# The last stage of a two-layer decoder step, turned into token rows before the scale and the residual instead of after them

## The reference, cut to what matters

```python
def rms_norm(x, g):
    xf = x.astype(jnp.float32)
    y = xf * lax.rsqrt(jnp.mean(xf * xf, axis=-1, keepdims=True) + NORM_EPS)
    return (y * g.astype(jnp.float32)).astype(x.dtype)
...
    o = rms_norm(o.astype(h.dtype), norm_g).reshape(B, T, GLA_VW) * jax.nn.silu(gate)
    h = h + rms_norm(o @ w_out, post_g)
    return h, st
```

## Time and profile before

| | us |
|---|---|
| three runs | 2061.0, 2062.63, 2062.9 (median 2062.63) |
| the profiled execution, its own time | 2063.2 |
| its span, first to last record | 2061.3 |
| PE busy / PEld busy in the span | 1959.9 (95%) / 1840.8 (89%) |
| DVE / ACT / POOL busy | 827.3 (40%) / 644.0 (31%) / 688.1 (33%) |
| mean granted TensorE clock | 0.967 of full speed |

### The profile page before, as it was taken

The page is one execution under the profiler, slowest core; times in us unless marked ns, Lnnn a source line. Parts: engine busy times, 40 slices in busy tenths (PEclk is TensorE's granted clock), DMA queues, the critical chain, the costliest instruction groups (busy, mean ns, idle before and its releaser), DMA issues.

```text
span 2061.3 us, 38375 instructions
## 1 busy us (share of the span) xinstructions
PE 1959.9 (95%) x14973; PEld 1840.8 (89%) x14973; DVE 827.3 (40%) x1478; ACT 644.0 (31%) x1158; POOL 688.1 (33%) x304
## 2 busy tenths in 40 slices
PE   6999999999999998999889999999999999989997
PEld 6998998899889987999779988988998899879996
DVE  5376337625742665100341454054316422650004
ACT  5232223222221233222342343334225332442122
POOL 2333332223323321545213314322341333225451
PEclk9999999999999999999999999998999899979998
DMA  5655245424533443522324352444244424533322
GB/s 167 200 159 153 73 118 159 127 82 136 157 94 95 142 142 98 171 84 83 91 91 124 113 168 79 123 138 150 75 121 154 134 72 138 180 138 103 101 83 83
DMA packets 357436, 252.53 MB, mean 123 GB/s; under 512 B 15136, under 2 KB 324785, under 8 KB 356721
## 3 DMA queue, kind: packets, MB, share of 16 engines
q1 hardware_dynamic: 316364, 186.75, 31.4%
q10 hardware_dynamic: 40900, 63.42, 9.2%
HBM read 213.62 MB, written 36.96 MB: 122 GB/s over the span
## 4 chain that ended last, share of the span: by engine, by line
PE 77%; DVE 10%; issue 6%; ACT 3%; SPq 2%; DMA 1%; POOL 1%; ACTq 0%; DVEq 0%; POOLq 0%
PE proj L990 64%; PE scratch L990 8%; PE score L990 2%; PE scratch L993 2%; DVE kv L1516 1%; DVE xlo L1388 1%; DVE probw L1544 1%; SPq L467 1%; SPq L459 1%; DVE ek L1787 1%; ACT ek L864 1%; POOL wlo L555 1%; DVE mix L1700 0%; DVE tz L1377 0%; DVE enew L1575 0%
## 5 line engine op out<-in xcount | busy, mean ns | idle before, releaser
L990 PE MATMUL proj<-xhi,wlo 128*128 128x268 f32 x4096 | 1198.0, 292 | 14.7 <-POOL wlo L555 6.3
L990 PE MATMUL proj<-xlo,whi 128*128 128x268 f32 x4096 | 1187.2, 290 | 0.0
L990 PE MATMUL proj<-xhi,whi 128*128 128x268 f32 x4096 | 1186.7, 290 | 0.0
L555 POOL TENSOR_TENSOR wlo<-wraw,whi 128x1024 fp32r<-128x1024 f32 x258 | 634.5, 2469 | 1133.7 <-ACT whi L621 1133.7
L990 PEld LDWEIGHTS proj<-xhi,wlo 128*128 128x128 f32 x4096 | 787.0, 192 | 32.9 <-issue 22.5
L990 PEld LDWEIGHTS proj<-xlo,whi 128*128 128x128 f32 x4096 | 786.4, 192 | 0.8
L990 PEld LDWEIGHTS proj<-xhi,whi 128*128 128x128 f32 x4096 | 783.7, 191 | 0.0
L621 ACT ACTIVATE whi<-wraw 128x1024 fp32r<-128x1024 f32 x258 | 265.1, 1047 | 383.3 <-PE proj L990 278.7
L1377 DVE TENSOR_TENSOR tz<-proj,rstd 128x536 f32<-128x536 f32 x72 | 51.4, 713 | 294.8 <-PE proj L990 294.4
L1695 DVE TENSOR_SCALAR mix<-proj,cols 128x536 f32 x32 | 24.8, 776 | 340.2 <-ACT te L627 179.5
L730 ACT ACTIVATE probw<-score,small 128x128 f32<-128x128 f32 (+3 forms) x64 | 33.2, 524 | 171.5 <-DVE small L1467 171.5
(11 more groups left out here) (267 smaller groups left out, 1747.6 us busy)
## 6 DMA issues: line engine op xcount, KB each, us to landing
wraw<-in_w_in SPq DMA_DIRECT2D x192, 512.0 KB, 4.0
wraw<-in_w_out SPq DMA_DIRECT2D x64, 512.0 KB, 4.0
kv<-in_cache_k SPq DMA_DIRECT2D x128, 128.0 KB, 2.3
kv<-in_cache_v SPq DMA_DIRECT2D x128, 128.0 KB, 2.3
sst<-in_state_gla ACTq DMA_DIRECT2D x32, 512.0 KB, 5.2
out<-sst ACTq DMA_DIRECT2D x32, 512.0 KB, 3.6
hbuf<-h_residual ACTq DMA_DIRECT2D x2, 4288.0 KB, 14.6
vb<-v_sample_rows ACTq DMA_DIRECT2D x32, 256.0 KB, 5.5
```

The costliest lines, as they stand in the source:

```text
L555: pool.tensor_tensor(wlo[:, slot, :, 0:width], wraw[:, kc, :, 0:width], whi[:, slot, :, 0:width].bitcast(F32), ALU.subtract).then_inc(s_lo, 1)
L990: return pe.matmul(out, lhsT, rhs, start=start, stop=stop, skip_group_check=True)
```

## The change

Three things change, all in the last stage of layer 1.

1. **Sums of squares per token row.** `token_sums` replaces `sum_squares(3)`: the squares are now the stationary operand (five groups of tokens) and one column of ones is the moving one, so that each token's sum lands on its own partition, in columns 0 to 4 of `score`. The ten matmuls (five from `acc`, five from `te`) add to what stands there: DVE zeroes the five columns beforehand. This `memset` stands in DVE's program behind the last `x_lo` of out1, and PE waits for it (s_zero) ahead of the whole projection. ACT forms Ln and Exp on 128 x 5 instead of 128 x 536.
2. **Transposes of raw data.** PE transposes both the unscaled output (`mix`) and the residual (`hbuf`), 20 pieces each, into a pair of banks for each piece, four pairs in turn. ACT copies the turned residual to the row buffer. The first two residual pieces are turned between the two halves of the sums; the other pieces follow as residual, output, residual, output.
3. **One DVE pass for each piece.** On the turned rows the scale is one value for each partition: `scalar_tensor_tensor`, row buffer = output x rstd + row buffer, 20 passes of 128 x 512. The 32 passes over channel blocks and the 20 result copies go.

```diff
@@ SP, result stores
-                sp.wait_ge(*result_read(i))
+                sp.wait_ge(s_res, i + 1)
@@ new helper
+        def pieces(i):
+            two = [(scratch[0][:], scratch[1][:]), (proj[1][:, 0, :], proj[1][:, 1, :]),
+                   (proj[0][:, 0, :], proj[0][:, 1, :]), (score[:, 0:512], score[:, 512:1024])]
+            return two[i % 4]
@@ ACT
             out_stage(3, N_OUT1, False)
-            finish_rms(3)
-            for i in RESULT_ACT:
+            def turned_h(i):
                 w = P if i % 5 < TT else TB
-                act.wait_ge(s_fT, i + 1)
+                act.wait_ge(s_fH, i + 1)
                 if i >= 15:
                     act.wait_ge(s_yout[1], 16 * 6)
-                act.copy(y_buffer(i)[0:w], banks[i % 8].rearrange("p (k e) -> p k e", k=4)[0:w]).then_inc(s_fa2, 1)
+                act.copy(y_buffer(i)[0:w], pieces(i)[1][0:w].rearrange("p (k e) -> p k e", k=4)).then_inc(s_hc, 1)
+            for i in range(2):
+                turned_h(i)
+            act.wait_ge(s_ss, 4)
+            chain.link(act.activation(stat[:, 2:7], score[:, 0:5], ACT.Ln, scale=1.0 / D, bias=eps))
+            act.activation(stat[:, 8:13], stat[:, 2:7], ACT.Exp, scale=-0.5).then_inc(s_rstd, 1)
+            for i in range(2, 20):
+                turned_h(i)
@@ PE
             for s in range(GH):
                 head(s)
+            pe.wait_ge(s_zero, 1)
             out_proj(N_OUT1, "out1")
-            sum_squares(3)
-            for i in range(20):
...
-                if i >= 8:
-                    pe.wait_ge(*result_read(i - 8))
-                for k in range(4):
-                    last = transpose(banks[i % 8][0:w, k * P:(k + 1) * P], mix[:, 4 * kq + k, tt * P:tt * P + w])
-                last.then_inc(s_fT, 1)
+            def token_sums(src, start):
+                for tt in range(TT + 1):
+                    w = P if tt < TT else TB
+                    last = matmul(score[0:w, tt:tt + 1], src[:, tt * P:tt * P + w], ones[:, 0:1], start=start and tt == 0, stop=not start)
+                return last
+            def turned(bank, i, src):
+                kq, tt = i // 5, i % 5
+                w = P if tt < TT else TB
+                for k in range(4):
+                    last = transpose(bank[0:w, k * P:(k + 1) * P], src[:, 4 * kq + k, tt * P:tt * P + w])
+                return last
+            pe.wait_ge(s_acc, 3 * KT - 1)
+            token_sums(acc, True)
+            pe.wait_ge(s_hld, 32)
+            for i in range(2):
+                if i == 1:
+                    pe.wait_ge(s_evac, N_OUT1 + KT + 1)
+                turned(pieces(i)[1], i, hbuf).then_inc(s_fH, 1)
+            pe.wait_ge(s_sq, 3 * KT)
+            token_sums(tef, False).then_inc(s_ss, 1)
+            for i in range(20):
+                if i in (2, 15):
+                    pe.wait_ge(s_evac, N_OUT1 + KT + 2)
+                if i == 3:
+                    pe.wait_ge(s_rstd, 4)
+                if i >= 2:
+                    if i >= 4:
+                        pe.wait_ge(s_hc, i - 3)
+                    turned(pieces(i)[1], i, hbuf).then_inc(s_fH, 1)
+                if i >= 4:
+                    pe.wait_ge(s_res, i - 3)
+                turned(pieces(i)[0], i, mix).then_inc(s_fT, 1)
@@ DVE
             x_lo("out1", 10, KT)
+            dve.memset(score[:, 0:5], 0.0).then_inc(s_zero, 1)
             out_stage(3, N_OUT1, POST1)
             dve.wait_ge(s_rstd, 4)
-            for k in range(KT + 1):
-                if k < KT:
-                    scaled(1, k)
-                if k >= 1:
-                    add_residual(1, k - 1)
-            for i in RESULT_DVE:
...
+            for i in range(20):
+                tt = i % 5
+                w = P if tt < TT else TB
+                y, h = pieces(i)
                 dve.wait_ge(s_fT, i + 1)
-                if i >= 15:
-                    dve.wait_ge(s_yout[1], 16 * 6)
-                dve.tensor_copy(y_buffer(i)[0:w], ...).then_inc(s_fd2, 1)
+                dve.wait_ge(s_hc, i + 1)
+                dve.scalar_tensor_tensor(out=y_buffer(i)[0:w], in0=y[0:w].rearrange("p (k e) -> p k e", k=4), scalar=stat[0:w, 8 + tt:9 + tt],
+                                         in1=y_buffer(i)[0:w], op0=ALU.mult, op1=ALU.add).then_inc(s_res, 1)
```

More of the change, by code:

```diff
@@ L48 @@
 PHYS = 40
-RESULT_DVE = [16, 18]
-RESULT_ACT = [i for i in range(20) if i not in RESULT_DVE]
 TILE_ORDER = [0, 4, 1, 2, 3]
@@ L214, in build @@
         s_yout = [sem("s_yout"), sem("s_yout_first")]
-        s_fT, s_fd2, s_fa2 = sem("s_fT"), sem("s_fd2"), sem("s_fa2")
+        s_fH, s_hc, s_fT, s_res, s_zero = sem("s_fH"), sem("s_hc"), sem("s_fT"), sem("s_res"), sem("s_zero")
         s_lam, s_v = sem("s_lam"), sem("s_v")
@@ L1348, in _ @@
                 head(s)
+            pe.wait_ge(s_zero, 1)
             out_proj(N_OUT1, "out1")
-            sum_squares(3)
-            for i in range(20):
+            def token_sums(src, start):
[4 more added lines that the diff above has]
+            def turned(bank, i, src):
                 kq, tt = i // 5, i % 5
                 w = P if tt < TT else TB
[L1355 to L1358, removed]
-                    pe.wait_ge(s_rstd, 4)
-                if i >= 8:
-                    pe.wait_ge(*result_read(i - 8))
-                for k in range(4):
-                    last = transpose(banks[i % 8][0:w, k * P:(k + 1) * P], mix[:, 4 * kq + k, tt * P:tt * P + w])
-                last.then_inc(s_fT, 1)
+                for k in range(4):
[14 more added lines that the diff above has]
+                if i == 3:
+                    pe.wait_ge(s_rstd, 4)
+                if i >= 2:
[5 more added lines that the diff above has]
+                turned(pieces(i)[0], i, mix).then_inc(s_fT, 1)
         @block.vector
@@ L1908, in _ @@
             x_lo("out1", 10, KT)
+            dve.memset(score[:, 0:5], 0.0).then_inc(s_zero, 1)
             out_stage(3, N_OUT1, POST1)
             dve.wait_ge(s_rstd, 4)
-            for k in range(KT + 1):
-                if k < KT:
-                    scaled(1, k)
-                if k >= 1:
-                    add_residual(1, k - 1)
-            for i in RESULT_DVE:
-                w = P if i % 5 < TT else TB
+            for i in range(20):
+                tt = i % 5
+                w = P if tt < TT else TB
+                y, h = pieces(i)
                 dve.wait_ge(s_fT, i + 1)
-                if i >= 15:
-                    dve.wait_ge(s_yout[1], 16 * 6)
-                dve.tensor_copy(y_buffer(i)[0:w], banks[i % 8].rearrange("p (k e) -> p k e", k=4)[0:w]).then_inc(s_fd2, 1)
+                dve.wait_ge(s_hc, i + 1)
+                dve.scalar_tensor_tensor(out=y_buffer(i)[0:w], in0=y[0:w].rearrange("p (k e) -> p k e", k=4), scalar=stat[0:w, 8 + tt:9 + tt],
+                                         in1=y_buffer(i)[0:w], op0=ALU.mult, op1=ALU.add).then_inc(s_res, 1)
 _INS = ["x_prompt", "x_sample", "cache_k", "cache_v", "state_pool", "state_gla", "page_table", "meta_tokens",
```

## The result

| | before | changed | ratio, 95% interval |
|---|---|---|---|
| median of 14 runs each | 2062.57 us (2058.3 to 2065.1) | 2071.38 us (2064.4 to 2073.6) | 1.0035 (1.0027 to 1.0044) |

The changed kernel is slower by 7.2 us by the ratio (5.6 to 9.1), 8.8 by the medians. Four executions of it have a profile. The first, shown here, ran 2071.88 us with a span of 2070.1; the others ran 2069.26, 2073.85 and 2062.62.

A forecast was written before the change was run, and what follows sets the result against it. PE's unbroken projection was taken as the bound, followed by a DVE-bound tail. The wait's 12.0 us less the tail's 7.05 gave +4.95 us, 2062.63 to 2067.6 us, range 2064.0 to 2070.8 us.

The forecast's parts named there:

- Part 1: Projection's start: PE waits for the memset; 0.7 us later start, 10.4 for 84 matmuls, 0.85 for the clock: +12.0 us.
- the clock after the restart: PE's first matmuls after idling before the projection: half level for 5.3 us, net cost 0.85 us, between 0 and 3.
- Part 2: Tail behind the projection: 23.35 us against 30.4, a gain of 7.05 us, turning from DVE-bound to PE-bound.
- The likeliest case: Whole kernel: wait +12.0, tail -7.05, full clock in the tail; +4.95 us, 2067.6 us, chance 0.57.
- rival A: Tail: the granted clock falls at the token sums, losing 1.6 us of transposes; +6.6 us, 2069.2 us, chance 0.25.
- that run: In the heads: some 2.7 us of small 16-column matmuls, behind which the clock fell; compared with 2.2 us of token sums.
- B: Tail: transposes do not hold the clock, 160 cost 34 us instead of 17.9; +21 us, 2083.7 us, chance 0.03.
- C: Projection's start: beside idle PE, DVE's last six xlo passes end 4.2 us sooner; +0.8 us, 2063.4 us, chance 0.06.
- D: Tail: transposes go faster than 0.11 us, so DVE bounds it at 0.66 a piece; +1.3 us, 2063.9 us, chance 0.04.
- the two restarts before: Earlier trace, from about 1832.2 and from 2040.44: half level for 5.3 us both times, a loss of 2.35 us.

The follow-up runs named there:

- e2: The kernel before plus only the memset behind the last xlo pass and PE's wait ahead of the projection, old tail kept: 2073.19 us, ratio 1.0046.
- e4: e1 with only one of the four transposes of each residual piece, the rest left out: 2052.77 us, ratio 0.9943 to the kernel before.
- e1: The changed kernel with PE's wait for the zeroed columns moved behind the projection: 2056.29 us, ratio 0.9966 to the kernel before; run for a second profile, 2054.74 us.
- e3: e1 with the token sums of acc issued inside the projection's last tile, between its halves: 2054.02 us, ratio 0.9963 to the kernel before.
- e7: e5 and e6 together, on e1: GpSimd's splits held and the residual fetched late: 2053.15 us, ratio 0.9958 to the kernel before.
- e5: e1 with GpSimd's weight splits for the second tile held until DVE's last xlo pass is done: 2053.02 us, ratio 0.9955 to the kernel before.
- e6: e1 with the residual fetched near the end of the projection instead of at its beginning: 2055.98 us, ratio 0.9969 to the kernel before.
- e8: e1 with every token sum issued twice, the copies going to unused columns: 2062.23 us, ratio 0.9998 to the kernel before.

## Why the prediction was right, and where its sizes were off

**The wait (Part 1).** Predicted +12.0 us, measured +11.5, by the middle of three profiles and by e2; +11.0 in the fourth. All are measured against before's one profile. The 84 matmuls are there by count. The start is 0.65 us late (8.27 us behind the first pass against 7.62; 0.7 predicted). The rest is the clock after the restart: 4.2 us at the half level instead of 5.3, 0.5 us less lost (4.6 in e2, 3.5 in the fourth profile).

**The tail (Part 2).** Predicted 23.35 us, measured 23.05 to 23.1 where the clock stays full. Sums 2.04 us (2.2), pieces 0.873 us (0.895), rstd ready 3.6 us behind the first sum (4.0) and waited for by nobody. DVE's pass 0.75 us. If PE were not the bound the tail would be 19.6 us, said the prediction; e4 gave 19.7.

**The likeliest case was the wrong one of two neighbours.** The point, +4.95 us, supposed a full clock behind the sums; rival A (0.25, +6.6) is what three of four profiles show. Its size came out as reckoned: 24.8 - 23.1 = 1.7 us (1.6). In these profiles the change costs 11.5 - 5.6 = 5.9 us. That is inside the measured 5.6 to 9.1, whose middle stays 1.3 us higher, and what makes up the difference is not shown. One candidate is in the record: before's profile had 3.35 us at the half level in the second tile, e1's second profile, with the same start of the projection, had none and was 1.5 us shorter there. Runs of the kernel before without that stretch would put the change's cost up to 1.5 us higher. By the ratio the time is inside the stated range (2069.8 of 2064.0 to 2070.8); the medians differ by 8.8, and 2071.38 is 0.6 us outside it. I mis-sized the chance of A: "it is shorter than that run, with transposes in between" was no ground for one in four.

**What is left.** The first of the six passes came between 1837.60 and 1846.82 us in the 14 profiles of this study, all with the same DVE code up to there (of PE's only the first tile of out1 is moved). The mean is 1842.4 for the four of the changed kernel and 1842.0 for the ten others, so no hand of the change is seen in it, and it spreads single runs by 9 us. Between before and the first profile after, 3.0 us of the 8.8 in span are this. Why the fall is frequent in the changed kernel and absent in seven profiles with the same or nearly the same tail (e1 twice, e3 to e7) stays open; four profiles are few.

**The rivals.** B is out: with nothing but transposes on PE the full clock held for 16.6 us in e1 (the stretch below, columns as above). The Trainium skill ("TensorE: Matmul & The Clock Gate", "Part 4: PE-mode transpose") states that the full clock does not engage in transpose mode; for these float32 transposes that does not hold.

```profile
2035.20:2051.80 16.60, 16.60 (x152) 15.95 (x152) 13.68 (x19) 10.67 (x20) 0.00 (x0) 1.00 0.63 220
```

C is out by e2 and by the trace itself (8.14 us with PE idle). What did stretch the passes is shown by e5: GpSimd's passes hold up DVE's (8.20 us against 3.85). The Trainium skill ("SBUF — State Buffer", "Who interferes with whom") says that a VectorE instruction with two SBUF inputs contends with a GpSimd one that reads SBUF, and e5 agrees. By e6 the DMA has no effect. D is out: the transposes cost 0.109 us each in the stream of e1 (0.873 a piece), not less.

## What to carry to other kernels

A semaphore wait costs what stands behind it in its engine's program, not what it protects: here a memset of 0.06 us, needed 180 us later, held back 84 matmuls, because it stood at the head of a stage built to start block by block. Put a wait directly ahead of its consumer, and place the producer before the long chain it has nothing to do with (the second half was not tried here). Then, when a stage changes from VectorE to TensorE, count TensorE's small matmuls as a risk to its clock, and judge a step of a few microseconds inside one trace, between two events that both kernels have.

## What the runs showed of the hardware

- A float32 matmul with one moving column costs about as much as one with eight: 1.02 us for five (2045.32 to 2046.34), 0.20 each, against four in 0.87, 0.22 each, in the earlier trace rows.
- Two-input DVE passes of 0.64 us from SBUF became up to 2.9 us each beside GpSimd's passes: six took 8.14 to 8.21 us in all eight kernels where they stood beside them, 3.85 in the two where they did not (e5, e7).
- After PE's idle 17.9 us the half level lasted 4.2 to 4.6 us more in four profiles (changed kernel, e2) and 3.5 in a fifth, not the 5.3 of the two restarts before. The same code can show it or not: 3.5 us in the second tile in one profile of e1, none in the other; 3.4 us in the tail in three profiles of the changed kernel, none in the fourth.
- The clock fell while PE was busy without a gap, with one-column matmuls alone (e8, whose second twenty run from 2032.10 to 2035.28: granted clock 0.86 from 2032.1 to 2033.0, 0.50 from 2033 to 2034), and transposes alone held it full for 16.6 us (e1).
